# Another order for the selection, the halves of the second query tile and the gate pieces in a hybrid trunk's sparse stage

## What is computed

```python
p_cmp = softmax(qb @ k_cmp - slope * dist) * ok      # 63 compressed blocks
o_cmp = p_cmp @ v_cmp
imp = p_cmp (summed over heads) @ overlap            # 32 selection blocks
idx = top_k(where(forced, 1e4, imp), 4)
o_sel = softmax(qb @ ks[idx]) @ vs[idx]              # selected blocks of 32 keys
o_win = softmax(qb @ kw_window) @ vw_window          # last 512 keys
o = g0 * o_cmp + g1 * o_sel + g2 * o_win
```

## Time and profile before

| | us |
|---|---|
| median of 3 runs | 1380.73 |
| lowest and highest run | 1376.51, 1380.79 |
| time of the profiled execution | 1376.33 |
| its span, first to last instruction | 1374.6 |
| PE busy in the span | 1311.0 |
| DVE busy in the span | 799.1 |
| POOL busy in the span | 602.1 |
| ACT busy in the span | 517.1 |

### The profile page before, as it was taken

How to read it: one execution, slowest core, us unless ns; L and a number is a source line. 1 busy time by engine, 2 the same in 40 slices (tenths; PEclk the granted TensorE clock), 3 DMA queues, 4 the chain that set the end, 5 groups by cost and what they waited for, 6 DMA issues and landing times.

```text
span 1374.6 us, 18689 instructions
## 1 busy us (share of the span) xinstructions
PE 1311.0 (95%) x7157; PEld 1056.0 (77%) x7157; DVE 799.1 (58%) x1289; ACT 517.1 (38%) x990; POOL 602.1 (44%) x395
## 2 busy tenths in 40 slices
PE   6999889999999989999999999999999999999998
PEld 5888556789787667666678888878888888888887
DVE  5896676633644876676626241287444543479952
ACT  6322554400122345554511110365445554463441
POOL 4213003134542310111148645267776777757662
PEclk9999999999999979999999999999999999999999
DMA  7530101031201310000155634151222211155334
GB/s 195 50 57 20 46 1 31 17 70 52 58 20 39 100 31 9 24 24 5 61 166 192 203 111 165 39 184 40 92 77 69 62 54 54 47 189 199 112 113 146
DMA packets 143673, 110.75 MB, mean 81 GB/s; under 512 B 41936, under 2 KB 116048, under 8 KB 143568
## 3 DMA queue, kind: packets, MB, share of 16 engines
q1 hardware_dynamic: 142784, 107.98, 26.8%
q10 hardware_dynamic: 800, 1.57, 0.5%
HBM read 86.33 MB, written 21.63 MB: 79 GB/s over the span
## 4 chain that ended last, share of the span: by engine, by line
PE 87%; DVE 7%; ACT 3%; issue 2%; DMA 0%; SPq 0%; ACTq 0%; DVEq 0%
PE ps L964 24%; PE ps L966 24%; PE ps L965 24%; PE ps L1506 2%; PE ps L1490 2%; PE ps L1222 1%; PE ps L1239 1%; PE ps L1471 1%; PE ps L1252 1%; PE ps L1473 1%; DVE merged L2304 1%; DVE hTl L2062 1%; PE ps L1083 1%; PE ps L1196 1%; PE ps L1422 1%
## 5 line engine op out<-in xcount | busy, mean ns | idle before, releaser
L964 PE MATMUL ps<-hTh,wh 128*128 128x512 f32 x784 | 314.5, 401 | 3.0 <-DVE hTl L2062 2.3
L966 PE MATMUL ps<-hTh,wl 128*128 128x512 f32 x784 | 306.2, 391 | 0.0
L965 PE MATMUL ps<-hTl,wh 128*128 128x512 f32 x784 | 305.9, 390 | 0.0
L924 POOL TENSOR_TENSOR wl<-raw,wh 128x512 fp32r<-128x512 f32 x162 | 235.3, 1459 | 154.7 <-ACT wh L1901 154.7
L828 POOL TENSOR_TENSOR wh<-raw,zero 128x1280 fp32r<-128x1280 f32 (+2 forms) x36 | 79.2, 2200 | 475.3 <-PE ps L966 471.3
L964 PEld LDWEIGHTS ps<-hTh,wh 128*128 128x128 f32 x784 | 147.6, 188 | 38.1 <-issue 9.3
L831 POOL TENSOR_TENSOR wl<-raw,wh 128x1280 fp32r<-128x1280 f32 (+2 forms) x45 | 128.8, 2862 | 103.1 <-ACT wh L1661 100.3
L964 PE MATMUL ps<-wh,hTh 128*128 128x512 f32 (+2 forms) x496 | 173.1, 349 | 0.0
L966 PE MATMUL ps<-wh,hTl 128*128 128x512 f32 (+2 forms) x496 | 173.0, 349 | 0.0
L965 PE MATMUL ps<-wl,hTh 128*128 128x512 f32 (+2 forms) x496 | 172.8, 348 | 0.0
L966 PEld LDWEIGHTS ps<-hTh,wl 128*128 128x128 f32 x784 | 147.3, 188 | 31.9
(11 more groups left out here) (377 smaller groups left out, 2336.8 us busy)
## 6 DMA issues: line engine op xcount, KB each, us to landing
raw<-in_w_in SPq DMA_DIRECT2D x35, 512.0 KB, 4.0
raw<-in_w_up SPq DMA_DIRECT2D x64, 256.0 KB, 2.8
arena<-in_w_down SPq DMA_DIRECT2D x32, 256.0 KB, 3.6
v_down<-arena SPq DMA_DIRECT2D x32, 256.0 KB, 2.6
raw<-v_down SPq DMA_DIRECT2D x32, 256.0 KB, 2.7
raw<-in_w_down SPq DMA_DIRECT2D x24, 256.0 KB, 2.9
merged<-in_x SPq DMA_DIRECT2D x8, 512.0 KB, 6.4
raw<-in_w_out SPq DMA_DIRECT2D x8, 512.0 KB, 3.8
```

What stands on the lines that cost most here:

```text
L924: eng.tensor_tensor(wlf[:, w_slot(n)], raw_piece(n), whf[:, w_slot(n)].bitcast(F32), ALU.subtract).then_inc(S("fw_split"), 1)
L964: mm(out_, ah, bh, start=first, stop=False, skip_group_check=True)
L965: mm(out_, ah, bl, start=False, stop=False, skip_group_check=True)
L966: return mm(out_, al, bh, start=False, stop=last, skip_group_check=True)
```

## The change

Only PLAN is changed. Nothing is added or taken away, and each instruction's work stays the same.

- soft 0 goes from ahead of F14 to behind F21, and split 0 from behind F21 to behind F19. Neither has work for PE, and ACT's order stays as it was; on DVE the order becomes: branch sums of panel 7 (F18, F19), remainders of the mixed heads, selection, branch sums of panel 8.
- F52 and F53 go ahead of pc 4 and pc 5, and each later gate piece up to F59 moves forward by one or two places between the pc and pvc entries, so that F54 follows pc 5 directly and F55 and F56 stand where F53 and F54 stood.
- qa 0, qb 0 and qa 1 come earlier by some entries: qa 1 now stands ahead of F59.
- F60 and qb 1 go from the loop (i = 17 and i = 2) to the last two places ahead of it.

```diff
@@ -413,17 +413,16 @@
         PLAN = [("cmp", 0)] + F(0) + [("cmp", 1)] + F(1) + [("cmp", 2)] + F(2) + [("cmp", 3)] + F(3)
         PLAN += [("q", n) for n in range(4)] + F(4) + [("q", 4), ("q", 5)] + F(5) + [("q", 6), ("q", 7)] + F(6)
         PLAN += [("kt", 0)] + F(7, 10) + [("cs", 0)] + F(10) + [("cs", 1)] + F(11) + [("cs", 2)] + F(12) + [("cs", 3)]
-        PLAN += F(13) + [("half", 0), ("half_exp", 0), ("soft", 0)] + F(14, 22) + [("split", 0)] + F(22, 37)
+        PLAN += F(13) + [("half", 0), ("half_exp", 0)] + F(14, 20) + [("split", 0)] + F(20, 22) + [("soft", 0)] + F(22, 37)
         PLAN += [("pc", 0), ("pc", 1)] + F(37) + [("pvc", 0), ("pc", 2)] + F(38) + [("pvc", 1), ("pc", 3)] + F(39) + [("pvc", 2)]
         PLAN += F(40) + [("mk", 0), ("pvc", 3)] + F(41) + [("half", 1)] + F(42, 44) + [("half_exp", 1)] + F(44) + [("soft", 1)] + F(45, 48)
-        PLAN += [("ka", 0), ("ka", 1)] + F(48, 51) + [("kb", 0), ("kb", 1)] + F(51)
-        PLAN += [("pc", 4), ("pc", 5)] + F(52) + [("pvc", 4), ("pc", 6)] + F(53) + [("pvc", 5), ("pc", 7)] + F(54) + [("pvc", 6)]
-        PLAN += [("mk", 1), ("pvc", 7), ("qa", 0)] + F(55, 57) + [("qb", 0)] + F(57, 60) + [("qa", 1)]
-        rest = fills[60:]
+        PLAN += [("ka", 0), ("ka", 1)] + F(48, 51) + [("kb", 0), ("kb", 1)] + F(51, 54)
+        PLAN += [("pc", 4), ("pc", 5)] + F(54) + [("pvc", 4), ("pc", 6)] + F(55) + [("pvc", 5), ("pc", 7), ("qa", 0)] + F(56)
+        PLAN += [("pvc", 6), ("mk", 1), ("pvc", 7), ("qb", 0)] + F(57, 59) + [("qa", 1)] + F(59, 61) + [("qb", 1)]
+        rest = fills[61:]
         TILE_AT = {row[0]: ROWS.index(row) for row in reversed(ROWS)}
         TILE_AT = {m: [i for i, piece in enumerate(PIECES) if piece[0] == row][0] for m, row in TILE_AT.items()}
-        PREP = {2: ("qb", 1)}
-        PREP |= {TILE_AT[m - 1] + d: (kind, m) for m in range(2, TB) for kind, d in (("qa", 1), ("qb", 4))}
+        PREP = {TILE_AT[m - 1] + d: (kind, m) for m in range(2, TB) for kind, d in (("qa", 1), ("qb", 4))}
         LAG_EXP, LAG_SCALE, LAG_T, LAG_PV, LAG_OUT = 1, 2, 5, 6, 7
         for i in range(NPC + LAG_OUT + 1):
             if i - LAG_SCALE in ROW_END:
```

## The result

| | before | after |
|---|---|---|
| median of 20 runs, us | 1378.35 | 1381.71 |
| lowest and highest run, us | 1376.24, 1382.84 | 1377.21, 1384.46 |
| ratio after to before, 95% interval | | 1.0024 (1.0016 to 1.0031) |
| time of the profiled execution, us | 1376.33 | 1382.53 |
| its span, us | 1374.6 | 1380.8 |

The change made the kernel 3.4 us slower by the medians (3.3 by the ratio), where the forecast was 0.6 us faster. PE does the same 7157 matmuls as before and is busy 6.4 us longer: the matmuls themselves took longer.

What follows compares the result with a forecast made beforehand. PE held 87% of the chain of last-ended waits, so only its waits or slow clock could give time. 0.0 + 2.3 - 1.4 - 1.5 = -0.6 us; forecast median 1380.1 us, range 1374 to 1386.

Steps and rivals of the forecast that it cites:

- A: Remainders of the mixed heads ahead of the first selection: PE's wait only moves to F29, worth 0.0 us.
- middle case: In A, POOL's split holds DVE's two-input product but not the reduction: F29 waits 3 us, worth 0.0 us.
- bounds: For A: F29 begins 1.3 us sooner without any hold by POOL, 1.3 us later if the reduction is held too.
- rival 1: Faster: waits go and none replace them, POOL's splits not holding DVE; clock staying up adds 2 us; 1374.1 us, chance 0.18.
- B: More gate pieces ahead of pc 4: F54's start unmoved, its wait about 5 us, F59's end 2.3 us later.
- C: Second query tile ahead of the loop: row maximum 2 comes sooner after F59's end, gain 1.4 us (bounds 4.1 and 0).
- D: F60 moved out of the loop to where PE runs it while DVE is busy: -1.5 us (bounds -1.5 and 0).
- the loss of gain that was cited against C: POOL waiting for qa 1's difference could end up to 0.5 us later, cutting C's gain to 0.9 us.
- Rival 3: Ahead of the loop, qa 1's difference loses to POOL: C gives 0, 1381.5 us, chance 0.12.
- Rival 2: Slower: 1.2 GHz lasts behind F54's wait, F55 to F59 run at half speed, 7.0 us more, 1387.1 us, chance 0.13.
- clock term of 2 us: In rival 1, the clock staying up from 494.2 to 508.8 us, at the loop's start, gives another 2 us.

Runs made afterwards that it cites:

- e3: The change without its part D (F60 and qb 1 left in the loop): median 1378.5 us, ratio to before 1.0000.
- e6: The change with 29 dense unused matmuls in four later loop waits, two waits there swapped in order: 1375.8 us, ratio to before 0.9982.
- e9: The kernel before with the same added lines as e6: 1376.02 us, ratio to before 0.9984.
- e15: The change with 8 dense unused matmuls in the loop where PE hardly waits, two waits swapped in order: 1376.4 us, ratio to before 0.9991.
- e7: The change with dense unused matmuls filling the loop's start: 1379.93 us, ratio to before 1.0012.
- e8: The kernel before with 10 dense unused matmuls in the wait ahead of F54: 1379.58 us, ratio to before 1.0008.
- e4: The change with 20 dense unused matmuls in the wait ahead of F54: 1375.02 us, ratio to before 0.9975.
- e10: The change with both the fill of e4 and the added lines of e6: 1374.35 us, ratio to before 0.9974.
- e5: The change again, unaltered, in another execution: 1381.34 us, ratio to before 1.0021.
- e14: Same as e15 but with 4 matmuls: 1380.01 us, ratio to before 1.0020.
- e16: Same as e15 but with 12 matmuls: 1381.21 us, ratio to before 1.0031.

## Why the prediction was wrong

**A: right.** Forecast 0.0, with a wait of 3 us moved to F29; it waits 2.80 us. The middle case was the true one. (By its own numbers the bounds are 1.5 us sooner and 1.2 later, not 1.3 each, and the rows that rival 1 calls five stretched ones are four; nothing hangs on either.) Timeline of DVE after:

```profile
416.73 2.36 DVE L2068 TENSOR_TENSOR br_l<-mixT,br_h 128x1024 fp32r<-128x1024 f32 x2 [0.34 <-ACT br_h L1803]
...
419.01 1.20 DVE L2446 TENSOR_REDUCE small<-arena 128x16 f32<-128x1008 f32 x1
...
420.53 2.45 DVE L2448 TENSOR_TENSOR arena<-arena,small 128x1008 f32<-128x1008 f32 x1
```

Both remainders at their free length, the reduction with one input not held, the product with two inputs held by POOL's split, which ran until 421.91: 2.45 us against 1.21 us.

**B and C: right in sum.** F54 waits 5.39 us (forecast about 5) and begins 2.39 us later than before, no later than everything ahead of the change does. Row maximum 2 comes at 498.54 - 492.18 = 6.36 us after the end of F59, forecast 6.3. Timeline of DVE:

```profile
492.12 0.68 DVE L2536 TENSOR_TENSOR q_low<-arena,merged_r 64x512 fp32r<-64x512 f32 x1 [2.15 <-ACT merged_r L1838]
...
493.56 1.98 DVE L2303 TENSOR_TENSOR merged<-merged,arena 128x512 f32<-128x512 f32 x1
495.46 0.47 DVE L2482 TENSOR_REDUCE small<-ps 128x1 f32<-128x128 f32 x2
...
496.46 1.83 DVE L2500 TENSOR_TENSOR small<-small,gates 128x1 f32<-128x1 f32 x1
498.33 0.28 DVE L2503 TENSOR_SCALAR arena<-arena,small 128x128 f32<-128x128 f32 x1
```

The difference of qa 1 won its race, the one-column product was held until POOL had finished. Timeline of POOL:

```profile
492.42 2.57 POOL L827 TENSOR_TENSOR wh<-raw,zero 128x1280 fp32r<-128x1280 f32 x1 [21.02 <-PE ps L965]
495.07 3.21 POOL L830 TENSOR_TENSOR wl<-raw,wh 128x1280 fp32r<-128x1280 f32 x1
```

POOL, second here, took 2.57 us for its first split instead of 2.32. The Trainium skill (SBUF — State Buffer, section "Who interferes with whom") has the one that starts first keep the shared port and the other one stand still; that agrees, at 0.25 us for an overlap of 492.80 - 492.42 = 0.38 us, half of the 0.5 that the prediction had worked out. So row maximum 2 came where the forecast had it, and the loss of gain that was cited against C did not show. Rival 3 did not happen.

**D: right in the sum, and the part that brought the loss.** The loop's start gained what was forecast (e3 against the change: 1.4 us). But F60 back in the loop (e3) takes 12 us of slow time away, and the falls that the change's profiles have and e3's has not are 100 us further on.

**The step that failed** is the sentence behind D, "The slow stretch at 1.2 GHz I leave as it is: the small matmuls in it are the same". With it the sum had no term for the clock: it took slow time as a property of the small matmuls at one place. The runs show 8 us more of it per run, worth 3 to 4 us, in waits of the later loop that the change does not touch (e6 and e9), and that a shift of 0.9 us takes away again (e15). Rows 3 show only the stretch of the change, and the fall at 689.8 us stood in the same profile, unread: the loop's later waits could lose the clock before already.

**Rival 2** had the right engine and sign and the wrong place. Behind F54's wait the clock was at 1.2 GHz until 481 us and back up for F55, which began at 481.64 us; its price of 7 us was never due. What the prediction cited of the Trainium skill (TensorE: Matmul & The Clock Gate, Part 1), that activity releases the throttled clock, the fills agree with: they held it at 1.00 (e6, e7, e8).

**Rival 1**: F29's wait and POOL's hold came as in the forecast, so it is out. Its clock term of 2 us for the loop's start is not settled: e7 can't tell, and where the profile has some 3.5 us less of 1.2 GHz there, row maximum 24 came 0.5 to 0.6 us sooner behind row maximum 0 (e4 against the change, e10 against e6).

## What to carry to other kernels

When an order is changed, the waits that remain are part of the price: look through the whole loop for waits of PE at which the profile's clock falls in any execution, and put work into them before tuning anything else; here four gate pieces moved into four waits were worth 7 us in before and 10 to 13 in the change, and no other order gained more than 2. Use the clock of every run, not one profile: a kernel whose sum comes out right can still lose through the clock far behind the change. A fill that helps proves little about its place until the same fill has been put into the other kernel and at another place, and until one has seen what else the edit does: here two waits changed places with it, worth 0.5 us in the change and 1.6 in before.

## What the hardware showed that was not expected

- Useless work can speed a kernel up: with 8 dense matmuls at a busy place the change was 4 to 5 us faster, with 4 and 12 it was not.
- Waits of 1 to 2 us cost the clock in one execution and not in the next: the profile of e5, the same kernel as after, has no fall near 604 us, though PE waits 1.77 us there in both.
- The same time at 1.2 GHz has different prices: 0.42 to 0.46 us per us behind row maximum 24, about 0.15 at the loop's start (0.5 to 0.6 us for some 3.5 us, e4 and e10).
- The order of two waits ahead of one matmul, both of which must be met, was worth 0.5 us at the loop's start (e6, e14, e15 and e16 took 32.5 us from row maximum 0 to 24, the change 33.1).
